# Second token block's input on ScalarE's queue with its squares on VectorE, gelu table named behind each exponential, picks weighed in twos

## The reference

```python
def rmsnorm(x, gain):
    xf = x.astype(jnp.float32)
    r = lax.rsqrt(jnp.mean(xf * xf, axis=-1, keepdims=True) + EPS)
    return (xf * r * gain.astype(jnp.float32)).astype(x.dtype)
...
h = rmsnorm(x, norm1_gain[l])
(aq, ak, av, mq, mk, mv, mi, mf, mo, gate_a, gate_m) = split_columns(h @ w_in[l])
...
x = x + mixed @ w_out[l]
x = x + peer_ffn(rmsnorm(x, norm2_gain[l]), peer_w_query[l], peer_sub_keys[l], peer_down[l], peer_up[l])
```

## Time and profile before

| | |
|---|---|
| median of three runs | 1270.98 us |
| the profiled execution's own time | 1269.91 us |
| its span, first to last instruction | 1268.2 us |
| PE busy / DVE / ACT / POOL | 1172.7 / 711.9 / 622.5 / 752.9 us |
| DMA, mean over the span | 301 GB/s |
| DMA rate in the slices from 285 to 790 us | 421 to 426 GB/s |

### The profile page before, as it was taken

The page is one execution under the profiler, slowest core; times in us unless marked ns, Lnnn a source line. Parts: engine busy times, 40 slices in busy tenths (PEclk is TensorE's granted clock), DMA queues, the critical chain, the costliest instruction groups (busy, mean ns, idle before and its releaser), DMA issues.

```text
span 1268.2 us, 15414 instructions
## 1 busy us (share of the span) xinstructions
PE 1172.7 (92%) x5672; PEld 818.9 (65%) x5672; DVE 711.9 (56%) x1512; ACT 622.5 (49%) x1344; POOL 752.9 (59%) x481
## 2 busy tenths in 40 slices
PE   9999999999998677787799798889999999999998
PEld 8987999965553233333355353443599998888887
DVE  5443135399686675766859678665546533422223
ACT  8586555544434232234424553554654675544442
POOL 7696668645553344554444445454247678788885
PEclk9999999999999898889999999999999999999999
DMA  8553446999999999999999999999524446565542
GB/s 278 193 197 117 149 151 240 370 376 426 425 424 424 424 424 424 424 424 425 424 421 425 424 424 424 416 418 424 218 88 159 134 137 196 167 199 194 181 157 100
DMA packets 121996, 381.78 MB, mean 301 GB/s; under 512 B 8512, under 2 KB 66880, under 8 KB 89152
## 3 DMA queue, kind: packets, MB, share of 16 engines
q0 software_dynamic: 36864, 268.45, 50.7%
q1 hardware_dynamic: 83584, 112.25, 26.7%
q10 hardware_dynamic: 1472, 0.09, 0.1%
HBM read 379.72 MB, written 1.05 MB: 300 GB/s over the span
## 4 chain that ended last, share of the span: by engine, by line
PE 65%; DMA 20%; DVE 7%; ACT 4%; POOL 2%; issue 1%; ACTq 0%; DVEq 0%; POOLq 0%
DMA rows_w<-peer_rows_in,arena 17%; PE ps L1140 15%; PE ps L835 13%; PE ps L864 8%; PE ps L1391 6%; PE ps L1444 4%; PE ps L1395 3%; PE ps L1193 3%; DVE rows_w L2527 3%; PE ps L1344 2%; PE ps L1369 2%; POOL rows_w L778 1%; DMA arena<-peer_rows_in,arena 1%; PE ps L1214 1%; ACT wgt L1770 1%
## 5 line engine op out<-in xcount | busy, mean ns | idle before, releaser
L565 POOL TENSOR_TENSOR w_lo<-ring,w_hi 128x1024 fp32r<-128x1024 f32 x178 | 434.1, 2456 | 160.1 <-ACT w_hi L559 160.0
L1140 PE MATMUL ps<-rows_w,diag 128*128 128x512 f32 x672 | 324.5, 622 | 57.1 <-ACT diag L1779 57.1
L778 POOL DMA_INDIRECT rows_w<-peer_rows_in,arena x168 | 195.4, 1163 | 233.5 <-PE ps L1140 196.9
L1140 PEld LDWEIGHTS ps<-rows_w,diag 128*128 128x128 f32 x672 | 128.1, 199 | 220.4 <-issue 136.6
L2527 DVE CUSTOM_DVE_ANT_0 rows_w<-rows_w,arena 128x1024 f32<-128x1024 f32 x168 | 203.5, 1224 | 103.3 <-DMA rows_w<-peer_rows_in,arena 102.7
L559 ACT ACTIVATE w_hi<-ring 128x1024 fp32r<-128x1024 f32 x178 | 184.1, 1058 | 105.2 <-PE ps L1395 45.5
L1768 ACT ACTIVATE gelu<-dots,rr 128x4 f32<-128x4 f32 (+2 forms) x91 | 27.0, 296 | 318.6 <-DVE dots L2527 318.1
L1140 PE MATMUL ps<-arena,diag 128*128 128x512 f32 x260 | 124.3, 607 | 13.6 <-ACT diag L1779 13.5
L778 POOL DMA_INDIRECT arena<-peer_rows_in,arena x66 | 76.0, 1151 | 59.6 <-PE ps L1140 51.2
L2527 DVE CUSTOM_DVE_ANT_0 arena<-arena 128x1024 f32<-128x1024 f32 x66 | 80.5, 1224 | 37.8 <-DMA arena<-peer_rows_in,arena 37.6
L1140 PEld LDWEIGHTS ps<-arena,diag 128*128 128x128 f32 x260 | 48.5, 194 | 75.0 <-issue 54.1
(11 more groups left out here) (468 smaller groups left out, 2042.6 us busy)
## 6 DMA issues: line engine op xcount, KB each, us to landing
ring<-w_in_in SPq DMA_DIRECT2D x38, 1024.0 KB, 5.2
ring<-w_ffn_gate_in SPq DMA_DIRECT2D x11, 1024.0 KB, 5.3
ring<-w_ffn_up_in SPq DMA_DIRECT2D x11, 1024.0 KB, 5.3
ring<-w_ffn_down_in SPq DMA_DIRECT2D x11, 1024.0 KB, 4.9
ring<-w_out_in SPq DMA_DIRECT2D x8, 1024.0 KB, 7.2
ring<-w_branch_attn_in SPq DMA_DIRECT2D x4, 1024.0 KB, 5.3
ring<-w_branch_mlstm_in SPq DMA_DIRECT2D x4, 1024.0 KB, 5.2
arena<-w_in_in SPq DMA_DIRECT2D x2, 2048.0 KB, 12.1
```

What stands on the lines that cost most here:

```text
L565: pool.tensor_tensor(lo_of(n, u)[:, t, 0:cols], raw_half(n, g)[:, t, 0:cols], hi_of(n, u)[:, t, 0:cols].bitcast(F32), ALU.subtract).then_i ...
L778: pool.indirect_dma_start(pick_row(p, 0, 2 * D), None, a["peer_rows"], bass.IndirectOffsetOnAxis(ap=idx[:, g // PH, j:j + 1], axis=0)).the ...
L1140: ins = pe.matmul(acc[:, c, :], diag[:, p % 4, :], pick_row(p, D + c * CW, CW), start=(p == first), stop=True, skip_group_check=True)
```

## The change

1. The second block of x is loaded from ACT's queue, as its first DMA, in place of SP's second. ACT's other four loads stand behind it.
2. The second block's sum of squares is made by DVE (`tensor_tensor_reduce`), as DVE's first instruction. ACT waits for `x1_squared` in place of making it. DVE scales the second block directly behind the first; the copy of the positions and the two products with the frequencies, which stood between them, come behind.
3. `gelu_steps` gives twos in place of fours for groups 10 to 14. (Groups 4 to 9 keep fours.)
4. A load of gelu's table is named behind each exponential or logarithm amid the picks, and one load of the table that holds logarithm and exponential ahead of `o_scale(0)`.

```diff
@@ gelu_steps
-            if g < 4:
+            if g < 4 or HG0 // TOPK <= g < NB * PH - 1:
                 return (2,) * (TOPK // 2)
@@ block.sync
-            for b in range(NB):
-                sp.dma_start(xres[:, b, :], a["x"][b * P:(b + 1) * P, :]).then_inc(sem(f"x_loaded{b}"), 16)
+            sp.dma_start(xres[:, 0, :], a["x"][0:P, :]).then_inc(sem("x_loaded0"), 16)
@@ block.scalar
+            act.dma_start(xres[:, 1, :], a["x"][P:2 * P, :]).then_inc(sem("x_loaded1"), 16)
             act.dma_start(raw_half(0, 0)[:, :, HALF:HALF + 2 * MH], w1[:, :, MI0:MO0]).then_inc(sem("unit_loaded"), 16)
...
             for b in range(NB):
-                act.wait_ge(sem(f"x_loaded{b}"), 16)
-                link(act.activation(xn1[:, b, :], xres[:, b, :], ACT.Square, accum_out=ss[:, b:b + 1]))
+                if b == 0:
+                    act.wait_ge(sem("x_loaded0"), 16)
+                    link(act.activation(xn1[:, 0, :], xres[:, 0, :], ACT.Square, accum_out=ss[:, 0:1]))
+                else:
+                    act.wait_ge(sem("x1_squared"), 1)
@@ o_scale
                 act.wait_ge(sem("osq_summed"), b + 1)
-                if b:
-                    act.preload_act_table_set(LOG_EXP)
+                act.preload_act_table_set(LOG_EXP)
@@ the loop over picks; the same line also behind gate_exp(1), log_f(0), o_scale(0), the later gate_exp and lb_exp(0)
                         norm_x2(1)
                         gate_exp(0, (1, 2))
+                        act.preload_act_table_set(GELU)
...
                     if (g, k) in DECAY_AT:
                         decay(DECAY_AT.index((g, k)), 0)
+                        act.preload_act_table_set(GELU)
@@ block.vector
+            dve.wait_ge(sem("x_loaded1"), 16)
+            dve.tensor_tensor_reduce(xn1[:, 1, :], xres[:, 1, :], xres[:, 1, :], 1.0, 0.0, ALU.mult, ALU.add, ss[:, 1:2]).then_inc(sem("x1_squared"), 1)
             scaled_x1(0)
+            dve.wait_ge(sem("x1_squared"), 1)
+            scaled_x1(1)
             dve.wait_ge(sem("pos_loaded"), 2 * 16)
...
             link(ins)
-            scaled_x1(1)
```

## The result

| | time, us | first pick's issue on POOL | last dot product on DVE |
|---|---|---|---|
| before | 1270.42 median of 12 (1269.95 to 1271.55); profiled execution 1269.91 | 254.47 | 897.88 |
| changed | 1273.66 median of 12 (1272.95 to 1274.56); profiled execution 1273.35, span 1271.6 | 257.78 | 901.29 |

The ratio is 1.0024, with a 95% interval from 1.0016 to 1.0032: 2.0 to 4.1 us slower, 3.2 by the medians. The forecast was 1271.2, with a range up to 1273.0; it was wrong, and the change of 3.2 us is more than the 2.5 that I had called measurable.

A forecast was written before the change was run, and what follows sets the result against it. The prediction took a chain of waits into a gapless PE to bound the start, and DMA engines at 1.01 the picks. 1269.91 + 0.2 + 0 = 1270.1, plus 1.07 to the median: 1271.2; range 1269.6 to 1272.7, widened to 1268.9 to 1273.0.

The forecast's parts named there:

- The picks, 0: Picks: edits lie beside DMA engines at 1.01, so 0 us, with bounds of -1.0 to +1.0.
- table loads on the path: Rival, start and picks: table loads and waits are on the path; 4.9 us won, 3.84 in picks, 1266.1; chance 0.07.
- thin queue: Rival, picks: a fuller queue of rows ends the dip at 416 GB/s, 1.0 us won; 1269.9; chance 0.08.
- case (b): Start: both blocks of x share the engines and land at 5.8; `hT_hi` at 9.65, 0.4 us later.
- 0.2 for the start: Start: summed term, 0.2 us lost, taken near the middle of 0.1 won to 0.6 lost.
- case (d): Start: gains, which `hT_hi` waits for, land at 9.8 at the worst, making `hT_hi` 0.6 us later.
- the gate columns land late: Rival, start: gate columns land at 11.9, ACT's first unit starts 3.9 us late; 1274.9; chance 0.08.
- ACT's first unit starts behind 8.5: Start: sign that the forecast is wrong, a load of ACT's queue being the new bound.
- 254.4 to 255.1: End of the start: sign that the forecast is right, POOL's first issue of a pick standing in this range, us.

The follow-up runs named there:

- e2: Only the picks' edits (twos in groups 10 to 14, named table loads) put into the kernel before; 1270.39 us, ratio 0.9998.
- e5: Kernel before with the changed start, but gate columns and gains on SP's queue between first block and weights; 1270.53 us, ratio 1.0001.
- e9: Whole changed kernel, with only gate columns and gains moved to SP's queue between first block and weights; 1270.58 us, ratio 1.0000 to the kernel before.
- e10: Kernel before with the changed start, ACT's queue reordered: second block, gains, gate columns, positions, frequencies; 1275.14 us, ratio 1.0038.
- e7: Kernel before with the changed start, ACT's queue reordered: gains, positions, frequencies, second block, gate columns; 1277.93 us, ratio 1.0060.
- e3: Kernel before with second block's squares on DVE and positions behind both scalings, its load still on SP's queue; 1271.16 us, ratio 1.0002.
- e6: Kernel before with only the second block's load moved to ACT's queue, both squares still on ACT; 1276.38 us, ratio 1.0048.
- e4: Kernel before with the changed start, but the second block's load last on ACT's queue; 1276.02 us, ratio 1.0041.
- e1: Only the start's edits put into the kernel before, picks as before; 1273.80 us, ratio 1.0026.

## Why the prediction was wrong

- **The picks, 0: right.** e2 puts them at -0.3 us (-1.4 to +0.9). DVE's last dot product still waits 1.19 us for its row, and ACT's loads are ahead of their waits. The rival "table loads on the path" is out, as it asked for 3.84 us. The "thin queue" asked for 1.0, which e2's times alone don't exclude; the profiles speak against it, as the stretch of the picks got no shorter (643.41 us before; 643.51 in the changed kernel, 644.20 in e2) with the rate at 424 to 425 GB/s where it had been 416.
- **The start, case (b): right.** It had both blocks at 5.8, the scaling at 7.7 and 8.6, `hT_hi` at 9.65. They were there at 5.8 and 6.0, the scaling ran from 7.62 to 9.3, and in e5 and e9, where the small loads are early, `hT_hi` stood at 9.53 and 9.66. That the last two fit so well is partly luck: there ACT's first unit, which starts at 8.47 and 8.64 when its weights land, ends just ahead of `hT_hi`, and the prediction had it start at 8.00. The sum took 0.2 for the start, not this case's 0.4.
- **The start, case (d): the step that failed.** "It is issued some 0.5 us later now and has 0.5 MB more ahead of it on its queue, 1.2 us at 425 GB/s: 9.8 at the worst." The gains landed at 12.52. It was issued 1.1 us later, not 0.5, as ACT's issues of positions and frequencies lasted 0.67 and 1.07 us. More than that, the way of counting was wrong: a load's own bytes and the bytes ahead on its own queue, while the other queue counted for nothing. The gate packets ahead of it and its own had to take turns with those of 46 to 90 ns on the other queue. The term was +0.6 at the worst and it measured 3.3: the gains alone, at 12.52, would hold `hT_hi` at 12.54 even if the unit were on time.
- **The rival "the gate columns land late": it came true, mis-sized.** Against it stood "alone on their queue they took 4.3 us, and 1.2 for the block ahead puts them at about 6.8". ACT's unit waited until 9.94. By the rival's own rule, one microsecond for each behind 8.0, that is 1.94, and the gains behind them add 3.31 - 1.94 = 1.4. It gave 1274.9 from the only row of a small load behind big ones, the 10.6 us of `ifbias`, and 0.08 was far too little for a mechanism with a row in its favour. The split of 1.9 and 1.4 is read along the path of one profile, and e10 failed to confirm it. That the rival's 3.9 us lies nearest to the measured 3.2 is partly luck: it had the unit 2 us too late and nothing for the gains.
- **"Right" and "wrong" signs.** "ACT's first unit starts behind 8.5 (then a load of ACT's queue is the new bound)" is what showed, and POOL's first issue left its 254.4 to 255.1.
- **The sum and its range.** The forecast stands on the median of three runs, 1270.98; the median of twelve is 1270.42, so 0.6 of its 1271.2 comes from the base and not from the change. And the range doesn't follow from its own terms: -0.1 - 1.0 - 0.5 and +0.6 + 1.0 + 0.5 on 1270.98 give 1269.4 to 1273.1, not 1269.6 to 1272.7. The measured 1273.66 lies outside both.

The prediction weighed a rule of the Trainium skill, "DMA: Bandwidth & Descriptors", section "Issuing engines are not separate DMA queues", by which the queues interleave on the same 16 engines. The trace agrees (659 packets beside 657). The prediction used it for the two large loads alone, where it forecast 0.4 us, and not for the small ones behind them, where it costs 3.

## What to carry to other kernels

Count a load that shares the engines with another queue by packets, not by bytes, while both queues have packets waiting: packets of its own and ahead of it on its queue, divided by the 16 engines, times one turn, which is little more than one packet of the other queue (49 ns here beside 1 KB, 89 beside 2 KB). The count gives the middle of the packets better than the last one (e10). A load of many short rows belongs in a stretch where the other queue moves nothing, or on the same queue ahead of the large load. When a load is moved to another queue, list all that stands behind it there, and what each waits for; here the cheap part was the load and the dear part a 64 KB and a 16 KB load behind it.

## What was not expected of the hardware

- Two queues were served packet for packet at all three sizes seen on SP's side: 48 packets of 4 KB beside 48 of 128 bytes (e7, 3.0 to 3.5 us, by the packets' records), 659 of 1 KB beside 657, 541 of 2 KB beside 543. It doesn't hold everywhere: in the kernel before, 1022 small ones left beside 67 from 3.5 to 4.5 us.
- Issuing a DMA on ACT lasted 0.67 and 1.07 us for positions and frequencies in the changed kernel, against 0.60 and 0.45 for the same two in e3, whose order on that queue is the old one. With the block ahead of them but no gate columns (e5) it was 0.46 and 0.60, with block, gains and gate columns ahead (e10) 1.18 and 1.15.
- The granted clock was 0.50 in the first stretches of six profiles: e3 and e10 from 9 to 11 us, e6 from 11 to 16, e4 and e7 from 11 to 17, e1 from 13 to 16. PE had been idle there for 1.86 and 2.08, 3.44, 5.27 and 4.30, and 2.08 us before it went on; in e4, e6 and e7 the clock fell within that idle time, from 10 us on. In the changed kernel, with idle times of 1.50 and 2.15, it stayed at 1.00, though e1 has the same start. So it can differ between kernels with the same start; each is one execution, and what decides is not shown. Of its price this much is seen: from `hT_hi` to POOL's first issue e1 and e3 took 0.4 us more than the 245.24 of the others, e4 0.9 and e6 1.3, but e7 nothing. In e3 it came to 1.1 us at the first issue, if e5 is taken as e3 without it (255.87 to 254.77).
